# Normalization split into two pairs of row blocks, statistics products moved within attention turns, and conditioning steps moved out of a down projection

## The chip, the cores and the metric

The kernel is one program on one core of a Trainium2 chip. The core has TensorE (PE), which multiplies matrices and transposes; VectorE (DVE), ScalarE (ACT) and GpSimd (POOL) for the rest; and SyncE (SP), which here issues every DMA. The engines run their own instruction lists and wait for each other by semaphores. The metric is the device time of the whole program in microseconds (us), the median of several runs; smaller is better.

## The reference, cut to what matters

All values are fp32. The input is x of 512 rows by 1024 columns, with 256 rows of context beside it in the first half. The first half (stages `ev` and `od`) has two mixer layers; the second half has layers 0 and 1, each a mixer and a feed-forward block. Every one of the four blocks of the second half starts with a normalization that is modulated by a condition c, and ends with a gated addition:

```
adaln(c):          mod = silu(c) @ w_mod + b_mod, split into 6: shift, scale, gate for mixer and for ffn
modulate(x,g,..):  rmsnorm(x, g) * (1 + scale) + shift
ffn:               x + gate * ((silu(h @ wg) * (h @ wu)) @ wd),   h = modulate(x),  wg, wu 1024 x 2816
mixer:             x + gate * (mix(h @ w_in) @ w_out),            h = modulate(x)
```

In stage `ev`, attention B subtracts two softmaxes, and its result has an rms norm of its own over each head's 128 values (the "sub norm").

## The kernel before, in words

**Stages.** They follow each other as: norm ev, proj A, attention A, proj B, attention B, out ev, norm od, proj M, attention M, proj N, attention N, out od, norm l0m, proj S, attention S, out l0, norm l0f, ffn l0, norm l1m, proj D, attention D, out l1, norm l1f, ffn l1. A name such as l0f is the norm ahead of the feed-forward of layer 0. One function per engine (`tensor`, `scalar`, `vector`, `gpsimd`, `sync`) writes out that engine's list by hand, in that order. There is no planner: the order of the code is the order of each queue, and a wait holds all that is behind it.

**Norm of the last four blocks** (`norm_last`, `norm_mod`, `round_h`, `lower`). The output projection before it (`out_proj`, or the end of `ffn`) makes x in four row blocks t of 128 rows, in two halves of 512 columns. For each: DVE gates and adds (`add`), ACT squares with a row sum (`norm_half`), POOL makes the reciprocal root (`norm_tile`), DVE scales the row block into WK (`norm_tile`, event xn t). Then PE transposes: for each of 8 column tiles f the row blocks 0, 1, 2 into one PSUM bank (24 transposes), and after xn 3 the fourth (8 transposes). DVE applies scale and shift out of PSUM, 128x512 per f (`mod_h`); ACT rounds it to fp32r (`hh`, the high part); the low part is the difference, odd f on DVE and even f on POOL (`hl`). Each product of the second half is done in three fp32r passes: high by high, high by low weight, low by high. `fm_first` is the first product behind the norm: 32 matmuls on the high parts as they come (2 outputs, 8 f, 2 passes), then 16 on the low parts.

**Weights.** They come through a ring of 4 buffers (`load` on SP, chunk i waits until PE is done with chunk i-4). ACT rounds a chunk (`round_chunk`), DVE or POOL takes the rest (`rest`).

**Feed-forward** (`ffn`). 22 turns f of gate and up products, then the down projection in two halves hh of 512 output columns, 22 tiles f each, for 4 row blocks. ACT makes the high part of the activation (`round_a`), POOL the low part (DVE for the last four of the second half). The last six f of the second half (38 to 43 in all, "kept") are done row block by row block, so that x comes out block by block.

**Conditioning steps** (`ada`, `ADA_STEPS`). The adaln products run beside everything else in 192 small steps: "chunk" (SP loads 512 KB, DVE does four multiply-adds of 128x256), "sum", "apply" (PE broadcasts or turns the sum; for gates ACT copies it to GATE). `FFN_STEPS` gives the steps per turn: three per turn in the 22 turns of ffn l0 and three after each of the 6 chunks of the first down half; one per turn in ffn l1.

**Attention B** (`attention`, `sub_norms`). 24 units of 128 queries and two heads, one per turn. PE in turn i: scores of unit i, transposes of the probabilities of unit i-2 into PSUM banks 4 and 5, then `extra`, then the products of unit i-3, then a piece of the next gate projection as filler (`FILL`). The 8 units in `B_DONE` (3, 5, 9, 11, 15, 17, 21, 23) end a sub norm: `extra` runs `sum_squares` in turn u+5 and `spread` in turn u+6. DVE has for the first a `diagonal` (with a power on POOL in its middle), for the second two multiplications, each after that turn's maxima.

Of the kernel before, what the change touches and what calls it, by code (L numbers as in the profile page):

```python
# [291 lines left out]
FFN_STEPS = {"l0f": (3, 3), "l1f": (1, 0)}  # L292
# [4 lines left out]
def program(nc, A, out_d):  # L297
    ctx = ExitStack()
    with ctx:
# [441 lines left out]

        def attended_by(tag, u, U):
# [19 lines left out]
        VA_TILES = (4, 5, 0, 1, 2, 3)  # L762

# [66 lines left out]
        def tensor(pe):  # L830
# [59 lines left out]
            def norm_last(st, by):  # L890

                for f in range(8):
                    b = next_bank(("turn", st, f, 0), by(f, 0))
                    for t in range(3):
                        pe.wait_ge(dve_value, ("xn", st, t))
                        pe.transpose(bank(b, t * 128, (t + 1) * 128),
                                     WK[:, t * 1024 + f * 128:t * 1024 + (f + 1) * 128], ident)
                for f in range(8):
                    pe.wait_ge(dve_value, ("xn", st, 3))
                    pe.transpose(bank(where["turn", st, f, 0], 384, 512), WK[:, 3072 + f * 128:3200 + f * 128], ident)  # L900
                    pe.then_inc(pe_turned, ("turn", st, f, 0))

# [27 lines left out]
            def fm_first(st, parts):  # L930

                for i, m, tag, t, by in parts:
                    next_bank(("p", tag, t, 0), by(0))
                for k in range(8):
                    pe.wait_ge(act_value, ("hh", st, k, 0))
                    for i, m, tag, t, by in parts:
                        (Wh, Wl), b, c = split_weights(i, 8), where["p", tag, t, 0], slice(m * 128, (m + 1) * 128)
                        pe.wait_ge(rest_signal(i), ("rest", i, k // 4))
                        pe.matmul(bank(b), Wh(k, c), Hh(st, k), k == 0, False)
                        pe.matmul(bank(b), Wl(k, c), Hh(st, k), False, False)  # L940
                for i, m, tag, t, by in parts:
                    Wh, b, c = split_weights(i, 8)[0], where["p", tag, t, 0], slice(m * 128, (m + 1) * 128)
                    for k in range(8):
                        wait_h(st, k, 0)
                        pe.matmul(bank(b), Wh(k, c), Hl(st, k), False, k == 7)
# [2642 lines left out]
```

## Time and profile before

| | us |
|---|---|
| median of 3 runs (lowest, highest) | 2376.01 (2374.91, 2379.13) |
| the profiled execution | 2372.06 |
| its span, first to last instruction | 2370.3 |
| PE busy | 2278.4 (96%) |
| DVE / ACT / POOL busy | 1301.3 (55%) / 788.9 (33%) / 331.9 (14%) |
| mean granted TensorE clock | 0.994 of full |
| stretches at half clock after the first 20 us | 102.8 (3.4 long), 529.5 (3.4), 1065.3 (6.8), 1614.9 (3.4), 1642.2 (3.4), 1754.8 (3.4), 2365.8 (6.5) |
| HBM read | 221.83 MB |

Times in a trace are us from the first instruction. "PE busy" counts a matmul from start to end although matmuls overlap, so 96% busy does not mean that PE is at its peak: what counts is the distance from one start to the next.

### The profile page before, as it was taken

What the parts mean: (1) busy time and instruction counts of PE and PEld (TensorE: products, weight loads), DVE (VectorE), ACT (ScalarE), POOL (GpSimd) and SP (SyncE); (2) the same over time, 40 slices, a digit from 0 to 9 for tenths busy, and PEclk for the clock granted to TensorE, in tenths of its full rate; (3) what the DMA queues carried; (4) which work ended last, traced back from release to release, by engine and by line L of the source; (5) the groups of instructions that cost most, each with busy time, mean ns of one, the idle gap of its engine ahead of it and who ended that gap; (6) DMA issues with size and microseconds to landing.
All of it is one profiled execution on the core that took longest, in us unless ns stands there. A gap on an engine that the chain in (4) does not pass through costs nothing.

```text
span 2370.3 us, 30353 instructions
## 1 busy us (share of the span) xinstructions
PE 2278.4 (96%) x11784; PEld 1722.5 (73%) x11784; DVE 1301.3 (55%) x2871; ACT 788.9 (33%) x1675; POOL 331.9 (14%) x333
## 2 busy tenths in 40 slices
PE   7999999989999999999999999999989999999997
PEld 5866576568645667787776888887767677888876
DVE  3565655655246654657767366666358844433333
ACT  4255103431112203623557122223433642222243
POOL 2200110001000112021200110003533002000154
PEclk9999999999999999999999999999999999999999
DMA  7200331002234363022310245554322102322321
GB/s 307 72 20 35 107 107 63 18 28 72 93 111 138 90 206 92 10 89 83 107 37 2 72 157 191 185 178 164 108 76 72 54 1 89 119 95 91 105 97 72
DMA packets 58267, 225.88 MB, mean 95 GB/s; under 512 B 20478, under 2 KB 21118, under 8 KB 41740
## 3 DMA queue, kind: packets, MB, share of 16 engines
q1 hardware_dynamic: 58124, 223.94, 28.2%
q8 instruction: 93, 1.52, 0.3%
q14 instruction: 50, 0.41, 0.1%
HBM read 221.83 MB, written 2.10 MB: 94 GB/s over the span
## 4 chain that ended last, share of the span: by engine, by line
PE 87%; DVE 5%; POOL 2%; ACT 2%; issue 1%; DMA 1%; SPq 1%; POOLq 0%; ACTq 0%; DVEq 0%
PE PS L86 82%; PE PS L91 5%; POOL WKr L103 1%; ACT WK L98 1%; DVE WK L108 1%; DMA GB<-in_ev_ada 1%; DVE WK L142 1%; SPq L162 1%; ACT WK L96 1%; POOL SM L103 0%; POOL Xr L103 0%; DVE X L103 0%; DVE ACC L115 0%; DVE WK L103 0%; ACT WKr L96 0%
## 5 line engine op out<-in xcount | busy, mean ns | idle before, releaser
L86 PE MATMUL PS<-Hr,GBr 128*128 128x512 f32 x1272 | 434.8, 393 | 2.2 <-ACT Hr L96 2.2
L86 PE MATMUL PS<-Hr,RINGr 128*128 128x512 f32 (+1 forms) x1048 | 405.6, 387 | 0.0
L96 ACT ACTIVATE WK<-PS 128x512 f32<-128x512 f32 (+2 forms) x391 | 189.1, 516 | 482.0 <-PE PS L86 290.2
L86 PE MATMUL PS<-H,RING 128*128 128x512 f32 (+1 forms) x928 | 336.3, 514 | 0.0
L115 DVE SCALAR_TENSOR_TENSOR ACC<-ADA,SM,ACC 128x256 f32<-128x256 f32 x608 | 297.1, 512 | 50.0 <-DMA ADA<-in_l_mod 30.8
L86 PEld LDWEIGHTS PS<-Hr,GBr 128*128 128x128 f32 x1272 | 237.8, 188 | 55.7 <-issue 3.4
L86 PEld LDWEIGHTS PS<-H,RING 128*128 128x128 f32 x928 | 172.0, 190 | 135.1 <-issue 126.9
L103 DVE TENSOR_TENSOR RINGr<-RING,GBr 128x1024 fp32r<-128x1024 f32 x148 | 182.5, 1271 | 145.5 <-ACT GBr L96 145.5
L86 PE MATMUL PS<-RING,GB 128*128 128x256 f32 x1152 | 252.6, 381 | 3.4 <-DVE GB L120 2.2
L86 PEld LDWEIGHTS PS<-RING,GB 128*128 128x128 f32 x1152 | 219.4, 191 | 34.7 <-issue 5.0
L86 PEld LDWEIGHTS PS<-Hr,RINGr 128*128 128x128 f32 (+1 forms) x1048 | 197.2, 188 | 40.6
L96 ACT ACTIVATE GBr<-RING 128x1024 fp32r<-128x1024 f32 (+1 forms) x154 | 154.3, 1046 | 200.3 <-PE PS L86 200.3
L86 PE MATMUL PS<-GBr,WKr 128*128 128x512 f32 (+1 forms) x664 | 213.2, 391 | 7.6 <-POOL WKr L103 7.3
L91 PE MATMUL PS<-CN,WK 128*128 128x128 f32 (+1 forms) x1104 | 162.4, 281 | 23.9 <-DVE WK L108 15.5
L86 PE MATMUL PS<-GB 64*128 64x256 f32 (+5 forms) x976 | 174.8, 437 | 10.9 <-DVE GB L120 2.9
L86 PE MATMUL PS<-Xr,GBr 128*128 128x512 f32 x456 | 174.4, 389 | 2.2 <-POOL Xr L103 2.2
L91 PEld LDWEIGHTS PS<-CN,WK 128*128 128x128 f32 (+1 forms) x1104 | 118.3, 140 | 79.6 <-DVE WK L108 31.4
L86 PE MATMUL PS<-WK,GB 128*64 128x128 f32 (+2 forms) x1856 | 158.6, 280 | 0.5 <-ACT EXQ L96 0.5
L86 PEld LDWEIGHTS PS<-GBr,WKr 128*128 128x128 f32 x664 | 126.1, 190 | 41.2 <-issue 13.7
L103 POOL TENSOR_TENSOR WKr<-GB,WKr 128x512 fp32r<-128x512 f32 x76 | 108.2, 1424 | 334.2 <-ACT WKr L96 331.2
L96 ACT ACTIVATE GB<-PS 128x256 f32<-128x256 f32 (+2 forms) x88 | 43.4, 493 | 316.7 <-PE PS L86 316.5
L86 PEld LDWEIGHTS PS<-GB 64*128 64x128 f32 (+1 forms) x976 | 84.2, 187 | 81.5 <-issue 57.3
(221 smaller groups left out, 2849.0 us busy)
## 6 DMA issues: line engine op xcount, KB each, us to landing
ADA<-in_l_mod SPq DMA_DIRECT2D x96, 512.0 KB, 3.8
RING<-in_l_gu SPq DMA_DIRECT2D x44, 1024.0 KB, 4.9
RING<-in_l_wd SPq DMA_DIRECT2D x24, 1024.0 KB, 4.9
RING<-in_ev_in SPq DMA_DIRECT2D x13, 1024.0 KB, 5.6
ADA<-in_od_ada SPq DMA_DIRECT2D x24, 512.0 KB, 3.6
RING<-in_od_in SPq DMA_DIRECT2D x11, 1024.0 KB, 6.1
RING<-in_l_in SPq DMA_DIRECT2D x10, 1024.0 KB, 4.9
RING<-in_l_out SPq DMA_DIRECT2D x8, 1024.0 KB, 5.3
```

The costliest lines, as they stand in the source:

```text
L86: self.last = self.eng.matmul(out, lhsT, rhs, start=start, stop=stop, skip_group_check=True)
L91: self.last = self.eng.transpose(out, in_, ident)
L96: self.last = self.eng.activation(out, in_, func, bias=bias, scale=scale)
L98: self.last = self.eng.activation(out, in_, func, bias=bias, scale=scale, accum_out=accum)
L103: self.last = self.eng.tensor_tensor(out, a, b, op)
L108: self.last = self.eng.tensor_scalar(out, a, s1, None, op0)
L115: self.last = self.eng.scalar_tensor_tensor(out=out, in0=a, scalar=s, in1=b, op0=op0, op1=op1)
L142: self.last = self.eng.tensor_tensor_reduce(out, a, b, scale, init, op0, op1, accum)
L162: self.last = self.eng.dma_start(out, in_)
```

## The change

1. **Sub norms of attention B.** `sum_squares` and `spread` run at the end of PE's turn, one turn number lower (u+4 and u+5). On DVE their partners run at the front of the next turn, ahead of the maxima.
2. **Values of attention A.** Row block 0 is projected in turn 0, 1 in turn 1 (before: both in turn 1); 2 and 3 stay in turn 2.
3. **Norms l0m, l0f, l1m, l1f in two pairs.** Pair 0 is the row blocks 0 and 1, pair 1 the blocks 2 and 3. The 16 transposes of pair 0 go behind the third row block's output product (in ffn l0 behind the first of the last six f of row block 3). DVE's scale and shift, ACT's rounding and the low parts of pair 0 (128x256 each) are done while the fourth block is multiplied. `fm_first` then starts with the transposes of block 2, multiplies pair 0, transposes block 3, and multiplies pair 1; its 48 matmuls of 512 columns become 96 of 256.
4. **Steps.** The three steps after each of six chunks of the down projection go. 3, 2, 1 and 0 steps are put behind the row blocks of out l0 (`OUT_STEPS`). Of the steps counted through the program, 6 now run in out l0, the 22 turns of ffn l0 end at step 182 instead of 176, and the last three of the nine steps that ran in the down projection run in the first turns of ffn l1.
5. **End of the down projection.** ACT rounds the kept activations 39 to 43 together at tile 38, ahead of the last weight chunk; DVE takes their low parts ahead of that chunk's rest. In ffn l0 ACT rounds chunk `l1_qi` ahead of the four squarings, and DVE takes its rest behind the first addition.
6. The weight of the final norm of the first half is loaded to GB in place of H, since H already holds pair 0 then.

The fence below holds the core of the diff; after the two tables and PE's part come ACT's lines (from `if fz < 38`), DVE's (from `def normed`) and SP's (the last).

```
-FFN_STEPS = {"l0f": (3, 3), "l1f": (1, 0)}
+FFN_STEPS = {"l0f": 3, "l1f": 1}
+OUT_STEPS = (3, 2, 1, 0)
+        PAIRS = ((0, 256), (256, 512))
+        VA_AT = {0: (0,), 1: (1,), 2: (2, 3)}
-            return [(u, step) for u in B_DONE for step in (0, 1) if i == u + 5 + step]
+            return [(u, step) for u in B_DONE for step in (0, 1) if i == u + 4 + step]
...
+            def pair_of(st, f, g, tiles):
+                for k in (f, f + 1):
+                    for t in tiles:
                         pe.wait_ge(dve_value, ("xn", st, t))
+                        pe.transpose(bank(where["turn", st, f, g], k % 2 * 256 + t % 2 * 128, k % 2 * 256 + t % 2 * 128 + 128),
+                                     WK[:, t * 1024 + k * 128:t * 1024 + (k + 1) * 128], ident)
+            def norm_early(st):
+                for f in range(0, 8, 2):
+                    next_bank(("turn", st, f, 0), [(dve_value, ("mod_h", st, f + 1, 0))])
+                    pair_of(st, f, 0, (0, 1))
                     pe.then_inc(pe_turned, ("turn", st, f, 0))
...
             def fm_first(st, parts):
+                norm_third(st)
                 for i, m, tag, t, by in parts:
                     next_bank(("p", tag, t, 0), by(0))
+                for g, (s0, s1) in enumerate(PAIRS):
+                    for k in range(8):
+                        pe.wait_ge(act_value, ("hh", st, k, g))
...
+                            pe.matmul(bank(b, s0, s1), Wh(k, c), Hh(st, k, s0, s1), k == 0, False)
+                            pe.matmul(bank(b, s0, s1), Wl(k, c), Hh(st, k, s0, s1), False, False)
+                    if g == 0:
+                        norm_fourth(st)
                     for i, m, tag, t, by in parts:
...
+                            pe.matmul(bank(b, s0, s1), Wh(k, c), Hl(st, k, s0, s1), False, k == 7)
...
-                        if hh == 0:
-                            ada(FFN_STEPS[st][1])
...
                         down(wd, 1, f, t)
+                        if t == 3 and f == 16 and st == "l0f":
+                            norm_early("l1m")
...
-            attention("B", sub_norms, at_end)
+                sub_norms(i)
+            attention("B", None, at_end)
...
+            def then_l0f(t):
+                ada(OUT_STEPS[t])
+                if t == 2:
+                    norm_early("l0f")
+            out_proj("l0_out", range(4), lambda k, t: None, then_l0f)
...
-                            round_a(fz + 1)
+                            if fz < 38:
+                                round_a(fz + 1)
+                            elif fz == 38:
+                                for kept in range(39, 44):
+                                    round_a(kept)
...
+                    act.wait_ge(pe_product, ("a_used", wd, KEPT - 1))
+                    round_chunk(FIRST["l1_qi"])
...
+            def normed(st, t):
+                if t == 2:
+                    scaled_pair(st, 0)
+                elif t == 3:
+                    lower_pair(st, 0)
+                norm_tile(st, t)
...
-                        for z in range(40, 44):
+                        for z in range(40, 44) if hh and cj == 4 else ():
...
-            attention("B", sub_norms)
+            attention("B", front=sub_norms)
...
             ada_until(ADA_AFTER["l0m", 5])
+            for n in OUT_STEPS:
+                ada(n)
             for j in range(4):
                 load()
```

## Rows read from the trace of the kernel before

**Rows 1.** The page: the chain that ended last, shares of the span by engine.
```profile
PE 87%; DVE 5%; POOL 2%; ACT 2%; issue 1%; DMA 1%; SPq 1%; POOLq 0%; ACTq 0%; DVEq 0%
```

**Rows 2.** The chain in order of time (start, length, what): ffn l0's 22 turns.
```profile
1370.39 241.40 PE PS L86 x1088
```

**Rows 3.** Timeline (start, length), PE in proj A: two 256-column fp32r matmuls in sequence.
```profile
62.99 0.28 PE L86 MATMUL PS<-GBr,WKr 128*128 128x256 f32 x1
63.11 0.28 PE L86 MATMUL PS<-Hr,RINGr 128*128 128x256 f32 x1
```

**Rows 4.** Timeline, attention B, turns 8 and 9 ([idle before <- what ended it]).
```profile
412.06 1.56 PE L86 MATMUL PS<-GB 64*128 64x512 f32 x8 [0.51 <-ACT WK L98]
...
413.55 0.88 PE L91 MATMUL PS<-CN,WK 128*128 128x128 f32 x6
...
414.96 1.05 PE L86 MATMUL PS<-CN,GB 128*128 128x1 f32 x8 [0.53 <-ACT WK L96]
...
416.38 1.02 POOL L103 TENSOR_TENSOR SM<-SM 128x4 f32<-128x4 f32 x1 [64.51 <-DVE SM L110]
...
417.44 0.88 DVE L108 TENSOR_SCALAR GB<-CN,SM 128x128 f32<-128x128 f32 x4 [1.23 <-POOL SM L103]
...
420.40 0.88 PE L91 MATMUL PS<-CN,WK 128*128 128x128 f32 x6 [0.62 <-DVE WK L115]
...
421.83 1.10 PE L86 MATMUL PS<-GB,CN 128*128 128x512 f32 x2 [0.56 <-ACT WK L96]
...
422.97 0.75 DVE L115 SCALAR_TENSOR_TENSOR EXQ<-EXQ,SM,PS 128x512 f32<-128x512 f32 x1 [0.89 <-PE PS L86]
```

**Rows 5.** Timeline, end of out l0, norm l0f and first product of ffn l0.
```profile
1343.69 29.66 SPq L162 DMA_DIRECT2D RING<-in_l_gu  x5
...
1353.86 2.78 PE L91 MATMUL PS<-CN,WK 128*128 128x128 f32 x24
...
1358.23 1.09 PE L91 MATMUL PS<-CN,WK 128*128 128x128 f32 x8 [1.59 <-DVE WK L108]
...
1360.40 0.47 PE L86 MATMUL PS<-Hr,GBr 128*128 128x512 f32 x1 [1.08 <-ACT Hr L96]
...
1363.20 7.14 POOL L103 TENSOR_TENSOR Xr<-X,Hr 128x512 fp32r<-128x512 f32 x2
...
1370.39 0.74 PE L86 MATMUL PS<-Xr,GBr 128*128 128x512 f32 x2 [1.13 <-POOL Xr L103]
```

**Rows 6.** Timeline, norm l0m: the fourth row block's transposes.
```profile
1064.80 1.49 PE L91 MATMUL PS<-CN,WK 128*128 128x128 f32 x8 [2.92 <-DVE WK L108]
```

**Rows 7.** Timeline, norm l1m: transposes of blocks 0 to 2, and of block 3.
```profile
1748.22 2.62 PE L91 MATMUL PS<-CN,WK 128*128 128x128 f32 x22 [2.12 <-DVE WK L108]
...
1752.25 1.09 PE L91 MATMUL PS<-CN,WK 128*128 128x128 f32 x8 [1.41 <-DVE WK L108]
```

**Rows 8.** Timeline, down projection of ffn l0: its start, and its second gate step.
```profile
1614.49 0.47 PE L86 MATMUL PS<-GBr,WKr 128*128 128x512 f32 x1 [2.71 <-POOL WKr L103]
...
1639.53 0.60 ACT L96 ACTIVATE GATE<-PS 128x512 f32<-128x512 f32 x1 [2.94 <-PE PS L86]
...
1641.64 0.47 PE L86 MATMUL PS<-GBr,WKr 128*128 128x512 f32 x1 [2.15 <-POOL WKr L103]
```

**Rows 9.** Stretches: length, busy PE, PEld, DVE, ACT, POOL, clock, DMA, GB/s.
```profile
1065.40:1072.10 6.70, 5.10 (x15) 3.86 (x14) 6.61 (x10) 4.44 (x8) 3.86 (x3) 0.50 0.32 105
...
1642.20:1645.60 3.40, 3.40 (x10) 2.66 (x9) 2.88 (x2) 0.34 (x1) 0.67 (x1) 0.50 0.94 361
1754.90:1758.20 3.30, 3.30 (x9) 2.52 (x9) 3.30 (x6) 2.86 (x6) 3.11 (x3) 0.50 0.00 0
```

**Rows 10.** Timeline, down projection of ffn l0, row block 0 of the kept tiles.
```profile
1730.63 0.47 PE L86 MATMUL PS<-GBr 128*128 128x512 f32 x1 [1.80 <-DVE GBr L103]
```

**Rows 11.** Groups by form: 128x256 out of PSUM on DVE, 128x256 low parts on POOL.
```profile
L120 DVE COPY GB<-PS 128x256 f32<-128x256 f32 x22 | 9.3, 422 | 51.6 <-PE PS L86 51.6
...
L103 POOL TENSOR_TENSOR GBr<-GB,Hr 128x256 fp32r<-128x256 f32 x7 | 7.6, 1084 | 22.5 <-ACT Hr L96 22.3
```

More of the change, by code:

```diff
@@ L1192, in ffn @@
                         chunk_done(FIRST[wd] + hh * 6 + cj)
-                        if hh == 0:
-                            ada(FFN_STEPS[st][1])
-                turn["set"] = list(range(8))
+                turn["set"], turn["at"] = list(range(4)), 3
                 for t in range(4):
@@ L1553, in tensor @@
             ada_until(ADA_AFTER["l1m", 3])
-            norm_last("l1m", lambda f, gi: [(dve_value, ("mod_h", "l1m", f, gi))])
-            close(of_pe, "norm l1m")
             def weights_i():
@@ L1686, in round_h, with round_pair @@
                 round_chunk(SECOND[st])
+            def round_pair(st, g):
+                a, b = PAIRS[g]
+                for f in range(8):
+                    act.wait_ge(dve_value, ("mod_h", st, f, g))
+                    act.activation(Hh(st, f, a, b), Hl_plain(st, f, a, b), ACT.Copy)
+                    act.then_inc(act_value, ("hh", st, f, g))
+                if g:
+                    round_chunk(SECOND[st])
             def copy_out(tag, t, s0, n):
@@ L2026, in scalar @@
                     ada(1)
+                if t == 2:
+                    round_pair("l0m", 0)
             cur.allowed |= {"l0f"}
@@ L2395, in weigh, with attention @@
                         dve.then_inc(dve_probs, ("probs", tag, u))
-            def attention(tag, extra=None, behind=None):
+            def attention(tag, extra=None, behind=None, front=None):
                 units, n, lag = UNITS[tag], len(UNITS[tag]), LAG[tag]
                 for i in range(n + 6):
+                    if front is not None:
+                        front(i)
                     for t, s0, m in filled(tag, i):
@@ L2620, in sub_norms @@
             def sub_norms(i):
-                for u, step in diff_steps(i):
+                for u, step in diff_steps(i - 1):
                     t, s0, n = UNITS["B"][u]["done"]
@@ L2885, in vector, with normed_with_steps @@
             since(dve, "att S")
-            out_proj("l0_out", "l0m", range(4), ("c2",), lambda t: norm_tile("l0f", t), "l0_gu")
+            def normed_with_steps(t):
+                normed("l0f", t)
+                ada(OUT_STEPS[t])
+            out_proj("l0_out", "l0m", range(4), ("c2",), normed_with_steps, "l0_gu")
             cur.allowed |= {"l1m"}
@@ L2890, in vector @@
             since(dve, "out l0")
-            ffn("l0f", "l0_gu", "l0_wd", lambda t: norm_tile("l1m", t))
+            ffn("l0f", "l0_gu", "l0_wd", lambda t: normed("l1m", t))
             cur.allowed |= {"l1f"}
@@ L2951, in vector @@
             since(dve, "att D")
-            out_proj("l1_out", "l1m", range(4), ("c2",), lambda t: norm_tile("l1f", t), "l1_gu")
+            out_proj("l1_out", "l1m", range(4), ("c2",), lambda t: normed("l1f", t), "l1_gu")
             close(of_dve, "out l1")
@@ L3216, in gpsimd, with then_l1m @@
             since(pool, "out l0")
-            ffn("l0f", "l0_gu", "l0_wd", lambda t: norm_tile("l1m", t))
+            def then_l1m(t):
+                norm_tile("l1m", t)
+                if t == 2:
+                    lower_pair("l1m", 0)
+            ffn("l0f", "l0_gu", "l0_wd", then_l1m)
             cur.allowed |= {"l1f"}
```

188 lines of the change are left out of this document (100 added, 88 removed).

## The prediction

> **What bounds the kernel now.** First the page: the chain that ended last is 87% TensorE, then DVE with 5% [rows 1]. So the time is PE's instruction list plus its waits, and a part of the change is worth what it takes from either. Then the chain in order of time, which gives PE's undisturbed rate: 1088 matmuls in 241.40 us, 0.222 us each [rows 2]. Against that rate I walked PE's starts through the whole trace and kept every distance that is too long. They lie in few places, and for these I read the timeline. The reader is to see three things there.
>
> (a) Each of the four late norms makes PE wait three times: for the fourth row block's xn (1.59 us idle), for the first rounded tile (1.08), and for POOL's low parts (1.13) [rows 5]; l1f repeats this to 0.03 us. (b) Where PE's work gets thin, the granted clock falls to half: 6.7 us in norm l0m, 3.3 to 3.4 us in l1m and at the second gate step of ffn l0's down projection [rows 9]. A half-clock stretch costs half of PE's busy time in it. (c) In attention B the small products of the sub norm wait 0.53 and 0.56 us behind ACT's copy of the transposes issued just before them, since both use banks 4 and 5 [rows 4].
>
> A wait costs more than its idle time: the last matmul's tail and the slow first one (0.47 long against 0.39) add about 0.2 to 0.25 us.
>
> **Sub norms of attention B.** The six transposes start at 413.55, 0.11 apart, so PE could go on at 414.25; it goes on at 414.96 [rows 4]: 0.7 lost. The starts before spread lose 0.72 to 0.78. Units 3 to 17 give 12 such waits, 8.7 us; units 21 and 23 fall into turns whose order stays the same. At the end of the turn the filler (1.9 us) has let ACT empty the banks, so these waits go. Beside this, scores wait 0.51 for the exponentials once in six turns [rows 4], where sum_squares will now stand: 3 x 0.67 = 2.0 more. And PE's wait of 0.62 for DVE's probabilities [rows 4], three times, should go as DVE no longer idles for the late sum: 1.8.
> What is added: DVE now has the diagonal ahead of the maxima. Queued behind it are the gate, the maxima and the weighing; ACT's exponentials wait for the maxima, and the next scores for ACT. The diagonal takes 0.2 + 1.02 on POOL + 0.2 + 0.88, the other half 0.75 + 0.69 (the add behind it) [rows 4]. Laying turns 8 and 9 out by hand, DVE ends its maxima 2 to 3 us later, and the next scores come 0.6 to 1 us late. I take 3.5 us for all. Nothing in the trace shows this order, so the bounds are 0 and 8.5. **Gain 8.7 + 2.0 + 1.8 - 3.5 = 9.0** (4 to 12.5).
>
> **Attention A.** 24 matmuls move from turn 1 to turn 0; PE has no long wait in either. Transposes come next in both orders after DVE has long made the probabilities. **0** (-0.5 to 0.5).
>
> **The four norms.** Before, the waits cost 1.59 + 1.08 + 1.13 and three times 0.23: **4.5 us** each in l0f and l1f. In l0m: 2.92 [rows 6], 1.6 idle in the half-clock stretch, 5.10/2 for its busy part [rows 9], 0.5 for the restarts: **7.5**. In l1m: 2.12 and 1.41 [rows 7], 1.07, 3.3/2 [rows 9], 0.7: **7.0**. Together 23.5.
> After: 32 transposes remain, 16 of them ahead of the fourth block's product, 0.11 each as now (2.78 for 24) [rows 5]; they move and cost nothing new. From the end E of the output product PE has block 2's transposes (0.9) and 32 matmuls of 256 columns. These start 0.12 apart [rows 3], so 3.85: PE is busy to E + 4.75, and xn 3 comes at E + 4.6 (1353.6 to 1358.2 in rows 5). The first wait is covered. Then the low products (1.9) cover DVE's and ACT's first tile of pair 1 (0.42 + 0.4) [rows 11], so the second goes too. The costs that take their place:
> - 96 x 0.12 = 11.5 in place of 48 x 0.222 = 10.7: 0.8 in each norm.
> - POOL's last low part. Before, two took 7.14 us where 2.6 would do [rows 5]: while DVE subtracted and took the chunk's rest, POOL's stood still, and it ended 1.1 after DVE's last. Now it starts about when DVE's own low parts start. If it gets ahead of them nothing is lost; if it falls behind the rest again, PE waits about 1.4. I take 0.7 in each norm.
> - l0f: SP now waits at block 2 for a conditioning chunk on DVE, which is behind eight scalings (8 x 0.42), a norm_tile (0.8) and four multiply-adds (2.0): from 1341.7 to 1348.2. Queued behind that wait is the first load of l0_gu, issued at 1343.69 now [rows 5]. It lands near 1353.2, ACT rounds it, DVE's rest comes ahead of the last addition, and xn 3 is 0.7 late.
> - l0m: the same eight scalings sit ahead of norm, final norm and a chunk; the last additions slip 1 us and the low parts of pair 0 0.2: 1.2.
> - l1m: the early transposes need xn 1 while PE reaches them 0.7 us after block 2's product; DVE and ACT are held by chunk l1_qi, which lands about 1732.4. I count 0.8 there and 0.3 for xn 2.
>
> So l1f 4.5 - 1.5 = 3.0; l0f 2.3; l0m 7.5 - 2.7 = 4.8; l1m 7.0 - 2.6 = 4.4. **Gain 14.5** (10 with POOL at its worst and 1.5 for other slips; 20.3 with the 0.8 alone).
>
> **Steps.** Counting the steps through the program, the gate applied in the down projection behind its second chunk is l1m 5. ACT cannot round on before it has copied this gate, which PE makes only then: ACT idles 2.94, PE 2.15 [rows 8]. With the restart and 3.4/2 for the half clock [rows 9] that is **4.0** (2.4 if the clock falls anyway). The wait at the projection's start has the same mechanism, 2.71 [rows 8], but there the count puts a gate into the 22nd turn in both kernels (l1m 4 before, l1m 5 after), so it stays. The other moved work is DVE's and SP's, covered by 5 us of DVE idle per half block of out l0 and by the turns of ffn l1; uncovered it would be at most 1 us. The applications cost PE the same elsewhere.
>
> **Kept tiles.** PE waits 1.80 [rows 10] as DVE's low parts stand behind the last chunk's rest, and ACT's roundings behind its chunk. Reordered, they are ready 2 us before they are needed, and the rest, at 1729.9, comes in time for tile 42. 2.05 in each of two projections: **4.1** (3 to 4.1). Next late is nothing of PE's.
>
> **Sum.** 9.0 + 14.5 + 4.0 + 4.1 = 31.6. The profiled execution took 2372.1 (its span and 1.8): 2340.5. The median of the runs is 3.9 above it, so 2376.0 - 31.6 = **2344 us**.
>
> **Rivals.**
> 1. *The chain through attention B eats its gain.* For it: scores already wait for ACT once in six turns. Against it: DVE's idle time there. Gain there 1 in place of 9: **2352**.
> 2. *POOL is locked out wholly.* The rows speak for it: POOL ended its last low part 1.1 us after DVE's last subtraction. The same in each of four norms costs another 0.7: 2344 + 2.8 = **2347**. By the Trainium skill, "SBUF — State Buffer", section "SBUF: two separate sides", a DVE operation with two SBUF inputs and a GpSimd operation hold a shared pair of ports exclusively, so that the later one blocks for the whole instruction. By that rule, the trace agrees (7.14 for two), and this rival is the case in which DVE always starts first.
> 3. *The start of the down projection is cured too*, by a gate copy that comes earlier: 2.71, restart and 3.4/2 of clock, 4.6 more: **2339**. Against it: the count of steps. Its opposite is the change not doing what it says: gates still copied between chunks.
> 4. *Slower.* DVE's diagonal and its second half lie open on the loop scores, maxima, exponentials, scores: 2.3 + 1.44 = 3.8 us at each of 8 units, 30 us, against a gain of 22.6 elsewhere: +7.8, **2384**. It decides from 2.8 us per unit. Against it: the tail's units are not in the loop, and DVE is 67% busy there (88.6 of 133 us).
>
> **How the numbers follow.** Forecast 0.63, rival 1 0.15, rival 2 0.12, rival 3 0.08, rival 4 0.02. The range takes the bounds of the terms, not all at once: gains of 16 (rival 1's 1 in attention B, norms 10, the rest 5.4) to 43. So 2333 to 2360, which holds rivals 1 to 3. A measurement of this kernel can tell about 0.2%, 4.8 us, from no change. Only rival 4 and a third of the outer misses reach that side: faster 0.94, same 0.03, slower 0.03.
>
> **What would show it.** In the changed kernel's profile: no half-clock stretch in l0m, l1m and behind the second chunk of ffn l0's down projection, but one near its start with some 2.7 us of idle; matmuls of 256 columns 0.12 apart behind each norm, with a wait before POOL's last low part under 1.5; CN,GB and GB,CN products in attention B without an ACT wait, its 133 us stretch about 124; no 1.8 us wait in the kept tiles. Wrong would be: 256-column matmuls that start 0.19 apart (the length of a weight load), scores waiting over 1 us in turns u+6, or the first row block's chain in ffn l0's end late by more than the 4.1 us that a block takes.

## The result, and the profile after

| | before | changed |
|---|---|---|
| median (lowest, highest), 4 runs each | 2375.46 (2372.75, 2379.13) | 2336.89 (2335.19, 2341.98) |
| the profiled execution, its span | 2372.06, 2370.3 | 2341.98, 2340.2 |
| mean granted TensorE clock, profiled | 0.994 | 0.994 |

The ratio is 0.984, 95% interval 0.9819 to 0.9861: 38.6 us less. Timed again, beside other kernels, it gave 2338.34 against 2371.21, ratio 0.9849 (0.9827 to 0.9872). The forecast was 2344, a ratio of 0.9867: direction and range hold, and the gain is some 4 to 7 us larger than forecast. The changed kernel's profiled execution is the longest of its four, so the two traces differ by 30.1 only; why is shown below.

**Where the time went.** I measured between the same matmuls in every trace: each mark is the start of the last matmul ahead of a long distance that all traces have at that place. Times in us; e1, e2 and e7 are runs described below.

| from, to | before | changed | changed again (e7) | attention B alone (e1) | norms undone (e2) |
|---|---|---|---|---|---|
| end of norm ev, attention B | 325.71 | 325.74 | 324.12 | 331.73 | 331.74 |
| attention B | 152.89 | 140.65 | 140.67 | 140.64 | 140.68 |
| its end, attention M | 202.56 | 202.56 | 202.56 | 202.55 | 202.55 |
| attention M, attention N | 186.76 | 189.74 | 186.45 | 186.67 | 186.45 |
| attention N, out od | 87.57 | 87.73 | 87.82 | 87.70 | 88.69 |
| out od, norm l0m, attention S | 195.76 | 193.03 | 193.07 | 195.36 | 196.46 |
| attention S | 99.95 | 99.88 | 99.88 | 99.94 | 99.96 |
| out l0, norm l0f, ffn l0 to its down projection | 314.02 | 313.26 | 313.21 | 313.99 | 316.93 |
| down projection, norm l1m, to attention D | 246.16 | 235.34 | 235.25 | 245.88 | 237.85 |
| attention D to the end | 512.96 | 505.86 | 505.84 | 512.85 | 510.77 |

The chain of the page answers to [rows 1], and the long chain of ffn l0 to [rows 2]. Here the chain could be followed back to 1350 us only, so its shares are of 42% of the span and say little against before's.

```profile
PE 38%; POOL 2%; DVE 1%; ACT 1%; issue 0%; DMA 0%; POOLq 0%; ACTq 0%; DVEq 0%
```

Attention B, turns 8 and 9, timeline (start, length, engine, line, operation, [idle before <- what ended it]):

```profile
411.88 0.95 PE L86 MATMUL PS<-CN,GB 128*128 128x1 f32 x8
...
412.75 1.56 PE L86 MATMUL PS<-GB 64*128 64x512 f32 x8
...
413.63 1.02 POOL L103 TENSOR_TENSOR SM<-SM 128x4 f32<-128x4 f32 x1 [61.28 <-DVE SM L110]
414.25 0.87 PE L91 MATMUL PS<-CN,WK 128*128 128x128 f32 x6
414.69 0.88 DVE L108 TENSOR_SCALAR GB<-CN,SM 128x128 f32<-128x128 f32 x4 [1.23 <-POOL SM L103]
...
416.21 1.99 PE L86 MATMUL PS<-H,RING 128*128 128x256 f32 x8 [0.65 <-DVE GB L115]
...
418.04 1.02 PE L86 MATMUL PS<-GB,CN 128*128 128x512 f32 x2
419.08 1.56 PE L86 MATMUL PS<-GB 64*128 64x512 f32 x8
...
420.57 0.87 PE L91 MATMUL PS<-CN,WK 128*128 128x128 f32 x6
```

Against [rows 4] the three waits for ACT and the one for DVE's probabilities are gone. One new wait came: the filler at 416.21 waits 0.65 for DVE's gate, which now stands behind the diagonal. Scores (419.08) come without a wait. Six turns, from scores to scores, took 34.91 us in the trace of before (407.46 to 442.37) and take 31.18 here (407.95 to 439.13).

Norm l0m, timeline of DVE and PE around the fourth row block (against [rows 6]):

```profile
1051.59 1.23 DVE L103 TENSOR_TENSOR RINGr<-RING,WKr 128x1024 fp32r<-128x1024 f32 x1 [1.74 <-ACT WKr L96]
1052.24 1.04 PE L91 MATMUL PS<-CN,WK 128*128 128x128 f32 x8
1052.73 1.22 DVE L103 TENSOR_TENSOR RINGr<-RING,GBr 128x1024 fp32r<-128x1024 f32 x1
1053.87 0.68 DVE L103 TENSOR_TENSOR WK<-PS,GATE 128x512 f32<-128x512 f32 x1
...
1059.41 1.09 PE L91 MATMUL PS<-CN,WK 128*128 128x128 f32 x8 [2.31 <-DVE WK L108]
```

The output product ends at 1052.2, but DVE first takes the rest of the next weight chunk, so the last gated addition starts at 1053.87 and xn 3 is 2.31 us late. In this trace the granted clock then falls to half from 1060.4 for 3.4 us. The six traces with this same code and this same wait (2.30 to 2.34) do not agree on that: the fall comes in the changed kernel, e4 and e7, and not in e3, e6 and e11. First the changed kernel, then e3 (length, busy PE, PEld, DVE, ACT, POOL, clock, DMA, GB/s):

```profile
1060.40:1063.80 3.40, 3.40 (x18) 3.40 (x18) 3.31 (x8) 2.19 (x6) 1.52 (x3) 0.50 0.52 158
```

```profile
1055.40:1058.80 3.40, 3.40 (x31) 3.40 (x30) 3.31 (x8) 2.16 (x6) 1.49 (x3) 1.00 0.52 130
```

From out od to attention S it takes 192.96 to 193.07 us with the fall and 191.53 to 191.57 without it.

Norm l0f (against [rows 5]):

```profile
1345.34 2.36 DVE L103 TENSOR_TENSOR RINGr<-RING,GBr 128x1024 fp32r<-128x1024 f32 x2 [5.55 <-ACT GBr L96]
...
1346.71 0.36 PE L86 MATMUL PS<-Hr,GBr 128*128 128x256 f32 x1 [0.59 <-DVE RINGr L103]
...
1352.06 1.09 PE L91 MATMUL PS<-CN,WK 128*128 128x128 f32 x8 [1.28 <-DVE WK L108]
...
1355.59 0.75 POOL L103 TENSOR_TENSOR Xr<-X,Hr 128x256 fp32r<-128x256 f32 x1
1356.27 0.75 DVE L103 TENSOR_TENSOR Hr<-H,Hr 128x256 fp32r<-128x256 f32 x2
1356.49 1.81 POOL L103 TENSOR_TENSOR Xr<-X,Hr 128x256 fp32r<-128x256 f32 x1 [0.16 <-ACT Hr L96]
```

The waits for the first rounded tile and for the low parts are gone, as forecast; a short one for the weight's rest came, and the one for xn 3 stayed. POOL has three of its four low parts done when DVE's begin.

Norm l1m (against [rows 7]) and the start of the down projection of ffn l0 (against [rows 8]):

```profile
1599.63 0.60 ACT L96 ACTIVATE GATE<-PS 128x512 f32<-128x512 f32 x1 [5.70 <-PE PS L86]
1599.71 0.53 POOL L125 MEMSET ACC<- 128x512 f32 x1 [22.14 <-PE PS L86]
1600.12 1.14 ACT L96 ACTIVATE WKr<-GB 128x512 fp32r<-128x512 f32 x2
...
1602.30 0.47 PE L86 MATMUL PS<-GBr,WKr 128*128 128x512 f32 x1 [2.71 <-POOL WKr L103]
...
1725.33 1.86 PE L91 MATMUL PS<-CN,WK 128*128 128x128 f32 x15 [1.18 <-DVE WK L108]
...
1730.94 1.09 PE L91 MATMUL PS<-CN,WK 128*128 128x128 f32 x8 [0.32 <-DVE WK L108]
```

The second gate's wait between chunks is gone and the first one, 2.71, is still there, both as forecast. The kept tiles (against [rows 10]): DVE's four low parts now begin 3.5 us before PE comes to the kept tiles, and PE finds no wait there.

```profile
1707.44 4.67 DVE L103 TENSOR_TENSOR GBr<-GB,GBr 128x512 fp32r<-128x512 f32 x4 [3.39 <-ACT GBr L96]
...
1710.91 0.39 PE L86 MATMUL PS<-GBr 128*128 128x512 f32 x1
```

**The clock as an account of its own.** Each run comes with its mean granted clock, to 0.001. Where PE is busy throughout, a stretch at half clock costs half its length (128x512 matmuls start 0.43 apart at 1643 us of before's trace, 0.22 to 0.23 at full clock) and lowers the mean by the same share, so time x clock is the time at full clock. Where PE waits inside such a stretch, this counts the clock too high. For each kernel I take the mean over its runs; rounding moves a single run by up to 1.2 us, and the mean of several by less.

| kernel | runs | mean us | at full clock | the clock's cost |
|---|---|---|---|---|
| before, in three groups of runs | 11, 17, 11 | 2373.2, 2372.9, 2374.1 | 2356.2, 2355.9, 2355.8 | 17.0, 17.0, 18.3 |
| changed, in two groups | 4, 5 | 2337.7, 2338.2 | 2326.6, 2327.4 | 11.1, 10.8 |
| e1 attention B alone | 5 | 2362.5 | 2344.0 | 18.5 |
| e2 norms and values undone | 6 | 2359.5 | 2336.7 | 22.8 |
| e3 kept order undone | 4 | 2342.2 | 2332.3 | 9.9 |
| e4 no steps in turn 21 | 4 | 2330.3 | 2323.9 | 6.4 |
| e5 values alone | 12 | 2372.1 | 2355.1 | 17.0 |
| e6 values undone | 5 | 2344.2 | 2328.3 | 15.9 |
| e8 three cures | 4 | 2325.6 | 2321.0 | 4.6 |
| e9 round first | 5 | 2333.3 | 2325.9 | 7.4 |
| e10 attention B and values | 6 | 2358.7 | 2343.0 | 15.7 |
| e11 steps (3, 0, 0, 0) | 4 | 2329.4 | 2321.8 | 7.6 |
| e12 two cures | 4 | 2326.5 | 2320.6 | 5.9 |

The means at full clock repeat to 0.4 us for the kernel before and to 0.8 for the changed one; most of what varies between executions of one kernel is the clock's part (17 runs of before: standard deviation 4.3 us as timed, 1.4 at full clock). A mean of the clock's part over five or six runs can be 1 to 2 us off. The change gains 29 us of the first kind and 6 of the second.

### The profile page after: what moved, and what is told of

Its sections match the earlier page's. It is cut to its first block and busy times, and to the rows that moved or that the text cites. A ratio compares the mean times of both kernels' runs of the same rounds, so it can differ in the third digit from the quotient of the medians.

```text
span 2340.2 us, 30852 instructions
## 1 busy us (share of the span) xinstructions
PE 2274.7 (97%) x11976; PEld 1732.8 (74%) x11976; DVE 1309.9 (56%) x2919; ACT 795.4 (34%) x1707; POOL 326.5 (14%) x349
## 5 line engine op out<-in xcount | busy, mean ns | idle before, releaser
L86 PE MATMUL PS<-Hr,GBr 128*128 128x512 f32 (+1 forms) x1332 | 440.6, 384 | 0.6 <-DVE RINGr L103 0.6
L86 PEld LDWEIGHTS PS<-Hr,GBr 128*128 128x128 f32 x1332 | 247.7, 188 | 51.7 <-issue 3.9
L86 PEld LDWEIGHTS PS<-Hr,RINGr 128*128 128x128 f32 x1112 | 208.9, 188 | 38.0
L91 PE MATMUL PS<-CN,WK 128*128 128x128 f32 (+1 forms) x1104 | 163.2, 282 | 16.6 <-DVE WK L108 11.1
L86 PE MATMUL PS<-Xr,GBr 128*128 128x512 f32 (+2 forms) x484 | 176.1, 378 | 0.0
L86 PEld LDWEIGHTS PS<-WK,GB 128*64 128x64 f32 (+2 forms) x1856 | 126.9, 149 | 21.3 <-issue 20.2
```

What stands on the lines that cost most here:

```text
L86: self.last = self.eng.matmul(out, lhsT, rhs, start=start, stop=stop, skip_group_check=True)
L91: self.last = self.eng.transpose(out, in_, ident)
```

## The experiments

Ratios are to the kernel before, timed in the same group of runs on the same chip.

**e1: part 1 alone** (put on the kernel before: `u + 4 + step`, PE's `sub_norms(i)` at the turn's end, DVE's at its front).

> The kernel before with part 1 of the change alone (attention B's sub norms at the end of PE's turn, their DVE halves at the front of the next). Theory: this part alone takes the 12.2 us that the two traces show between the start of attention B and its end (372.15 to 512.81 in place of 371.67 to 524.56), because DVE had room for the diagonal ahead of the maxima. So the ratio to the kernel before is 0.995 (12 us less), no stretch outside attention B changes, and DVE's diagonal makes no score late. Rival: only the 9.0 us of the prediction belong to it and the other 3 come from part 2 or from the neighbours; then 9 us less.

Measured: 2361.58, ratio 0.9954 (0.9938 to 0.997), 11 us. Attention B takes 140.64 us in place of 152.89, to 0.03 us what the changed kernel takes, and no other stretch changes by its own work. At full clock 2356.2 - 2344.0 = 12.2. The theory holds, the 9.0 does not. Its trace shows one thing beside it: 331.73 us up to attention B in place of 325.71, with half clock from 104 to 121 us, in a stretch that part 1 does not touch. That led to e5 and e6.

**e2: norms undone** (the kernel before with parts 1 and 4, and of part 5 the kept tiles; the earlier rounding of chunk `l1_qi` is not in it and so counts with the norms here).

> The kernel before with parts 1, 4 and 5 (sub norms, steps, kept tiles), without the norms in pairs and without part 2. What the changed kernel gains beyond this one is the norms' share. Theory: the traces put 2.7 (l0m) + 0.8 (l0f) + some 3 to 5 each for l1m and l1f on the norms, so this kernel is 10 to 12 us slower than the changed one: 22 to 26 us faster than the kernel before, ratio 0.989 to 0.991. POOL's last low part in l0f is again over 5 us long, since DVE's subtractions run beside it. Rival: the prediction's 14.5 us for the norms stand, and this kernel is 17 to 19 us faster than before, with steps and kept tiles worth less than 8 together.

Measured: 2361.67, ratio 0.9939 (0.9922 to 0.9957), 14.5 us by the ratio, 13.7 by the means: both expectations miss. At full clock the kernel is 19.5 us under the kernel before, close to the rival's 17 to 19; the clock took 5.8 of them back. In its trace the steps behind out l0 leave less cover to the old norm l0f: the wait for the fourth row block grows from 1.59 [rows 5] to 2.88, and 6.8 us at half clock begin in it, at 1356.8.

```profile
1358.22 1.97 PE L91 MATMUL PS<-CN,WK 128*128 128x128 f32 x8 [2.88 <-DVE WK L108]
...
1363.33 7.17 POOL L103 TENSOR_TENSOR Xr<-X,Hr 128x512 fp32r<-128x512 f32 x2
```

So the parts lean on each other: moving the steps cost 2.9 us there (314.02 to 316.93) and the norms in pairs took it back. Changed against e2, trace by trace, the norms give 3.4 (l0m), 3.7 (l0f), 2.5 (l1m) and 4.9 (l1f: 3.9 by the first turns of ffn l1, and 1.0 scattered over what follows), together 14.5; at full clock 2336.7 - 0.9 (part 2) - 2327.0 = 8.8. The norms alone lie between e2 and e6 (below), which differ in nothing else: 2359.5 - 2344.2 = 15.3 by the means, of which 8.4 at full clock and 6.9 of the clock.

**e3: order of the kept tiles undone.**

```
-                            if fz < 38:
-                                round_a(fz + 1)
-                            elif fz == 38:
-                                for kept in range(39, 44):
-                                    round_a(kept)
+                            round_a(fz + 1)
```

and DVE's four low parts go back behind the last chunk's rest.

> The changed kernel with the kept tiles rounded one by one behind the last weight chunk, as before (part 5's first half undone). Theory: PE waits 1.8 us ahead of tile 40 in both projections again, 2.05 us with the restart, so 4.1 us slower than the changed kernel: ratio to before 0.986 where the changed one has 0.984. Rival: the late roundings make row block 0 late once and the early transposes of l1m hide it, so in ffn l0 nothing shows: 2 us.

Measured: 2342.2, ratio 0.9869 (0.9852 to 0.9885), 4.7 us over the changed kernel's 0.9849 of another group of runs. The intervals of the two overlap; what carries the reading is the traces, against e7 2.85 us more from the down projection to attention D and 2.02 more from there to the end, and the 4.9 us at full clock. The wait of 1.80 is back in both projections; the rival falls.

```profile
1707.78 0.47 PE L86 MATMUL PS<-GBr 128*128 128x512 f32 x1 [1.80 <-DVE GBr L103]
```

**e4: no steps in turn 21 of ffn l0** (`ada(FFN_STEPS[st] if (st, f) != ("l0f", 21) else 0)` on every engine).

> The changed kernel with no conditioning steps in the last of the 22 turns of ffn l0. The gate l1m 5 is then copied behind attention D. Theory: the wait of 2.71 us at the start of the down projection exists because ACT copies this gate, and POOL clears the sum, ahead of rounding the first activation. Without it PE goes on without a wait, and with its restart and half of the 3.4 us at half clock that is 4.6 us less than the changed kernel: ratio to before about 0.982. The gate's application at the end of attention D costs up to 1 us there. Rival: the first activation is late for its own reasons (the last tanh, the last product, POOL's low part of 1.35 us), and the wait stays above 1.5 us with the gate gone; then under 1 us less.

Measured: 2330.56, ratio 0.9818 (0.9803 to 0.9834). ACT now rounds the first activation right behind its own work, 4.7 us ahead of PE, and PE waits for nothing:

```profile
1586.77 1.14 ACT L96 ACTIVATE WKr<-GB 128x512 fp32r<-128x512 f32 x2
1587.54 2.97 POOL L103 TENSOR_TENSOR WKr<-GB,WKr 128x512 fp32r<-128x512 f32 x2 [17.02 <-ACT WKr L96]
1591.52 0.39 PE L86 MATMUL PS<-GBr,WKr 128*128 128x512 f32 x1
```

From the end of attention S to attention D it takes 542.71 in place of 548.59, 5.9 less, and from there to the end 0.98 more, where the gate's application now stands: 4.9 net. Against the changed kernel's 0.9849 of another group the ratios give 7 us, of which 3.5 are at full clock (2327.4 - 2323.9). The theory holds.

**e5 and e6: part 2 alone, and undone** (`VA_AT` and its three uses).

> The kernel before with part 2 alone: row block 0 of attention A's values is projected in turn 0. Theory (new): the prediction's 0 was wrong. PE is busy for 3.32 us of the stretch 100 to 105 in the kernel before and for 4.94 in the changed one; where it is thin the granted clock falls to half, for 3.4 us in the one trace and for 17.1 us in the traces of the two runs with part 2 undone. So with this part alone the start of attention B comes 2 to 7 us earlier than without it, no trace shows a half-clock stretch between 100 and 125 us, and the median is 3 to 6 us under the kernel before's. Rival: the half-clock stretches fall anywhere by chance, and the ratio is 1.000 within its interval.

> The changed kernel with part 2 undone. Theory: a half-clock stretch of 3.4 to 17 us at 100 to 122 us comes back, and the median is 3 to 6 us over the changed kernel's of the same call; the spread of its runs grows from about 2 to about 8 us. Rival: no difference beyond 1 us.

Measured: e5 2371.21, ratio 0.9996 (0.9982 to 1.001) in 12 runs; e6 2344.93, ratio 0.9874 (0.9852 to 0.9896), against 0.9849 for the changed kernel beside it, 6.6 us by the medians. The stretches of the trace (length, busy PE, PEld, DVE, ACT, POOL, granted clock, DMA, GB/s), first with part 2 undone (e6), then the changed kernel again (e7), then part 2 alone (e5):

```profile
100.00:105.00 5.00, 3.26 (x27) 2.86 (x28) 1.92 (x7) 2.17 (x7) 0.00 (x0) 0.85 0.00 0
105.00:110.00 5.00, 5.00 (x28) 4.72 (x26) 3.11 (x10) 2.10 (x6) 0.00 (x0) 0.50 0.02 3
```

```profile
100.00:105.00 5.00, 4.94 (x48) 4.57 (x48) 1.92 (x7) 2.45 (x8) 0.00 (x0) 1.00 0.01 3
105.00:110.00 5.00, 5.00 (x55) 4.60 (x51) 3.31 (x11) 2.10 (x6) 0.00 (x0) 1.00 0.00 0
```

```profile
100.00:105.00 5.00, 4.94 (x47) 4.64 (x47) 1.63 (x5) 0.72 (x2) 0.00 (x0) 1.00 0.00 0
```

PE was idle for a third of the stretch before the fall without part 2, and 28 matmuls run in 5 us in place of 55. The idle time is a single wait: the scores wait 1.68 us for DVE's row maxima. It stands in all four traces without part 2, and the half clock begins within 0.3 us of its end. With part 2 the 24 matmuls of row block 0 stand in its place. The timeline of before, then of e7:

```profile
99.73 1.15 PE L86 MATMUL PS<-GB 64*128 64x256 f32 x12
...
102.56 2.33 PE L86 MATMUL PS<-GB 64*128 64x128 f32 x16 [1.68 <-DVE SM L142]
```

```profile
100.62 1.15 PE L86 MATMUL PS<-GB 64*128 64x256 f32 x12
101.70 0.33 PE L86 MATMUL PS<-GATEr,Hr 128*128 128x128 f32 x1
...
104.52 1.37 PE L86 MATMUL PS<-GB 64*128 64x128 f32 x16
```

In the four traces without part 2 the way to attention B is 325.71 once and 331.7 three times; in the ten with it 322.5 to 325.7, 323.6 on the mean: 322.5 where no half-clock stretch lies on the way, and two of 3.4 us (at 50.1 and 128.6) in the first trace of the changed kernel, which is why its 325.74 looks like before's. Two more waits, 1.03 and 1.62 us ahead of transposes of later turns, stand between 122 and 129 us in both kernels' traces. So in the traces part 2 is worth 6.6 us, and on the changed kernel 6.1 on the mean (6.6 by medians), 0.9 of it at full clock. But on the kernel before it gained nothing beyond the noise: 0.8 at full clock, and the clock's cost of 17.0 is the same. The one trace of e5 has half-clock stretches at 49.9 and 930.5 us that the trace of before lacks; whether the fall moves there in general is not shown.

**e7: the changed kernel again.**

> The changed kernel itself, unchanged, as the yardstick for its variants on this chip, and for what its trace owed to chance. Theory: the first trace's extra 3.0 us between 715 and 905 us (a conditioning chunk that landed late, and a half-clock stretch behind it) do not come back, and the median is 2333 to 2338. Rival: they belong to the change and come back.

Measured: 2338.34 (2336.9 to 2339.44), ratio 0.9849 (0.9827 to 0.9872). Between attention M and N it takes 186.45 in place of 189.74: the 3.0 us over the kernel before's 186.76 were chance. They came once more in the fourteen traces, in e10 (189.72), again with half clock in that stretch. The median lies 0.3 over the range that was expected.

**e8: the waits that were left.** On the changed kernel:

```
-OUT_STEPS = (3, 2, 1, 0)
+OUT_STEPS = (3, 0, 0, 0)
...
-                        if t == 3 and f == 16 and st == "l0f":
+                        if t == 3 and f == 18 and st == "l0f":
...
                 for jj in range(2):
+                    if t == 3 and jj == 0:
+                        round_chunk(FIRST["l0_in1"])
                     act.wait_ge(dve_value, ("x", "od_out", t, jj))
...
-                    if t == 3 and jj == 0:
-                        round_chunk(FIRST["l0_in1"])
...
-                norm_half("l0f", t, 0, "l0_out")
                 if t == 3:
                     round_chunk(FIRST["l0_gu"])
+                norm_half("l0f", t, 0, "l0_out")
```

> The changed kernel with four edits aimed at the waits that its trace still shows: steps (3, 0, 0, 0) behind out l0, so that the last turn of ffn l0 has no gate and the first load of l0_gu is not held; ACT rounds the first chunk of the next product ahead of the last row block's squares in out od and out l0, so that DVE's rest stands no longer between it and the last addition; the early transposes of l1m two tiles later. Theory: start of the down projection 4.6 less 1.0 at the end of attention D; xn 3 of l0m 1.4 us earlier, of l0f 0.7 to 1.4 with the 0.6 wait for the rest; l1m 1.3. Sum 7.5 to 9.5 us under the changed kernel of this call. Rival: the waits move on to the next late thing (ACT's squares, POOL's root) and only the 3.6 of the gate remain.

Measured: 2325.9 (2324.38 to 2326.4), ratio 0.9796 (0.9774 to 0.9818), 12.4 us under the changed kernel beside it: 6.4 at full clock, 6.2 of the clock. The forecast of 7.5 to 9.5 left out part of the clock's gain. In norm l0f no wait over 0.4 us is left. In l1m one is, longer than before the edit and now for another row block:

```profile
1714.34 1.09 PE L91 MATMUL PS<-CN,WK 128*128 128x128 f32 x8 [1.67 <-DVE WK L108]
```

**e9: the chunk rounded first, in out od alone.**

> The changed kernel with one edit: in out od ACT rounds chunk l0_in1 ahead of the squares of the last row block's first half, not behind them. Theory: xn 3 of l0m is late because DVE's rest of this chunk (2.4 us) stands between the last product and the last addition, which the changed kernel's trace shows at 1053.87 with the product over at 1052.2. The wait of 2.3 us ahead of the fourth row block's transposes falls to 0.9, and with PE busier no half-clock stretch follows it, so 1.4 + 1.7 = 3.1 us under the changed kernel. Rival: the stretch at half clock comes anyway (it has come in three of four traces of changed kernels), and only 1.4 us are gained.

Measured: 2333.55 (2329.96 to 2336.91), ratio 0.9822 (0.9798 to 0.9847). DVE has the rest done before the product ends, and starts the last addition 0.3 us behind it:

```profile
1049.16 1.22 DVE L103 TENSOR_TENSOR RINGr<-RING,GBr 128x1024 fp32r<-128x1024 f32 x1
...
1050.71 0.69 DVE L103 TENSOR_TENSOR WK<-PS,GATE 128x512 f32<-128x512 f32 x1 [0.33 <-PE PS L86]
1055.45 0.75 DVE L108 TENSOR_SCALAR WK<-WK,SM 128x1024 f32<-128x1024 f32 x1 [1.26 <-POOL SM L103]
1056.26 1.09 PE L91 MATMUL PS<-CN,WK 128*128 128x128 f32 x8 [0.89 <-DVE WK L108]
```

The wait is 0.89 in place of 2.31, and no half clock follows. From out od to attention S it takes 190.12 in place of 193.07: 2.95, where 3.1 was expected. Only 1.4 of it is the edit's own: e3, e6 and e11, with the old wait and no half clock behind it, take 191.55. The other 1.5 is a half-clock stretch that came in three of the six traces with the old wait and in none of the three with the short one (e8, e9, e12); that leans to the theory and does not show that the edit removes it. The runs agree on the first part: 0.7 and 1.5 us at full clock, by the two groups of the changed kernel. Over the whole the medians give 4.8 us and the ratios 6; what is beyond this stretch is the clock elsewhere.

**e10: parts 1 and 2.**

> The kernel before with parts 1 and 2. Theory: part 2 is worth 6 us on the changed kernel and nothing on the kernel before; if it needs part 1's denser attention B to keep its gain, this kernel is 16 to 19 us faster than the kernel before, ratio 0.992 to 0.993, where part 1 alone gave 0.9954. Rival: part 2's gain on the changed kernel has to do with the later parts or with chance, and this kernel stands at 0.995 as part 1 alone.

Measured: 2359.48, ratio 0.9933 (0.9913 to 0.9953) against 0.9954 for part 1 alone. 5 us by the ratios, 3.8 by the means, 1.0 at full clock. That is just short of the 0.992 to 0.993 that was expected, and the intervals overlap (0.9938 to 0.997 for part 1 alone), so this leans to the theory and does not settle it.

**e11: the steps alone.**

> The changed kernel with one number changed: the steps behind the row blocks of out l0 are (3, 0, 0, 0) in place of (3, 2, 1, 0). It does two things: the last gate leaves turn 21 (4.9 us less, as the run without steps in turn 21 showed), and the first load of l0_gu no longer stands behind a conditioning chunk. Theory: the second is worth the 0.6 to 0.8 us that PE waits for DVE's rest in norm l0f and half of the 1.4 before the fourth block's transposes, so this kernel is 6.3 us under the changed one, 1.4 under the one without steps in turn 21. Rival: the rest still stands ahead of the last addition, and nothing is gained beyond the 4.9.

Measured: 2329.64, ratio 0.981 (0.9787 to 0.9833), against the changed kernel's 0.9849 some 9 us where 6.3 was expected, 5.6 of it at full clock (2327.4 - 2321.8); about 2 us under e4 by the ratio and 2.1 at full clock (2323.9 - 2321.8), where 1.4 was expected. With this edit alone both waits of norm l0f fall under 0.4 us. SP was what held the chunk of l0_gu, not ACT's order. In the trace of e9, whose steps are (3, 2, 1, 0), PE waits 0.65 and 1.28, in the changed kernel's 0.59 and 1.28.

**e12: e8 without the later transposes.**

> The run with three cures, less the later early transposes of l1m, which go back to the first of the last six tiles. Theory: that edit only moved PE's wait from xn 1 (1.3 us) to xn 2 (1.8 us), since DVE's eight scalings begin later and stand ahead of xn 2; so this kernel is equal or up to 0.6 us faster than the 2325.9 of that run, relative to the kernel before the same 0.9796 or a little less. Rival: the shift had gained its 1.3 us and the wait for xn 2 has another cause; then this one is about 1 us slower.

Measured: 2326.47, ratio 0.9797 (0.9774 to 0.982): the same as e8. The early transposes wait 1.15 for xn 1 and 0.31 for xn 2, where e8 waits for xn 2 alone. The wait had moved.

```profile
1709.01 1.86 PE L91 MATMUL PS<-CN,WK 128*128 128x128 f32 x15 [1.15 <-DVE WK L108]
...
1714.62 1.09 PE L91 MATMUL PS<-CN,WK 128*128 128x128 f32 x8 [0.31 <-DVE WK L108]
```

e8 and e12 are the fastest kernels here, 2.0% under the kernel before.

## Why the prediction was right, point by point

The forecast's own sum, split into work and clock (3.4/2 and 5.10/2 where its steps counted them), against what the runs give:

| step of the prediction | forecast, of it clock | measured at full clock | by |
|---|---|---|---|
| sub norms of attention B | 9.0, 0 | 12.2 | e1 |
| attention A | 0, 0 | 0.9 | e5, e6, e10 |
| the four norms | 14.5, 4.2 | 8.8 | e2, e7 |
| steps | 4.0, 1.7 | 2.4 | e1, e2, less kept |
| kept tiles | 4.1, 0 | 4.9 | e3, e7 |
| sum | 31.6, 5.9 | 29.2, and about 6 of clock | |

Without its clock the forecast holds 25.7 us of work; 29.2 were measured. The 5.9 of clock agrees with the measured 6, but not term by term: by the means the clock's cost goes from 17.0 to 18.5 with part 1 (e1), to 22.8 with steps and kept tiles (e2), down to 15.9 with the norms (e6) and to 11 with part 2 (e7). That the sum of these comes out near 5.9 is luck.

- **What bounds the kernel, and the reading by starts: right.** Every gain lies in a place where the distance between two starts had been too long. But the list of such places had a hole: attention A's.
- **Attention B: mechanism right, size 3.2 too small.** The failed term is the 3.5 us for DVE's longer chain. Laid out by hand it made the next scores 0.6 to 1 late; in the trace scores wait only twice, at the stage's start and as before (0.93 and 0.87), and the price is the filler's wait of 0.60 to 0.65, three times. The tail, counted at nothing as its order stays, gave another 1.1 us. Rivals 1 and 4 (DVE's chain eats the gain) are refuted: the stretch takes 140.62 to 140.68 us in all twelve traces with part 1.
- **Attention A: the step that failed.** "PE has no long wait in either" was the argument for 0, and it is false: in the kernel before the scores wait 1.68 us for DVE, up to 102.56, just where the 24 matmuls were moved to. They fill that wait, and the half-clock stretch that stands behind it in all four traces without part 2 is in none of the ten with it. The work is worth 0.8 to 1.0 us in the runs at full clock (e5, e6, e10) and 1.5 in the traces, where the way to attention B is 322.5 with no half clock in it and before's 325.71 less half of 3.4 is 324.0. What the clock adds is 5 us on the changed kernel (e6, e7) and nothing that can be seen on the kernel before (e5); why they differ stays open.
- **The norms: sum near, in part by luck, shares wrong.** Against e2 the traces give 14.5 and the means 15.3 (e6), forecast 14.5. But of work it is 8.4 to 8.8 where 10.3 was forecast, and of clock 6.9 where 4.2 was; l0f's 3.7 holds a half-clock stretch of e2's trace that before's lacks. l1f gave 3.9 by the first turns of ffn l1, where 3.0 was forecast: of the costs set against it, POOL's 0.7 did not come, for POOL was three low parts ahead of DVE when DVE began. l0m gave 2.7 against the kernel before in place of 4.8. The failed step is xn 3 "at E + 4.6", read from l0f and used for all four: l0m makes two norms, and in the trace of before its xn 3 lies 5.6 behind the product's end (1059.10 to 1064.74), which the cover of 4.75 does not reach. With the slip that was forecast at 1 and measured at 1.5 it waits 2.31, and in this trace a half-clock stretch stayed, against the first sign that the prediction named. Where it did not come (e3, e6, e11) l0m gave 4.2. e9 removes 1.4 of the wait. l1m gave 2.5 between these traces, and 4.2 with the 1.7 of a half-clock stretch at the start of the down projection that e2's trace lacks; 4.4 was forecast, with 0.8 for early transposes that wait 1.18.
- **Rival 2, POOL locked out: refuted as a cost.** The mechanism is there (next section), and the order took it off the path.
- **Steps: right.** At the second chunk the wait of 2.15 us is gone (0.17 is left), and the wait at the start is there to 0.01 us (2.71). Rival 3, the start cured too, did not happen by itself; e4 and e11 are that rival made true, and it is worth 4.9 in e4's trace, where 4.6 was forecast. The 1.7 of clock in this term is not seen in the runs, where e2's clock costs 4.3 more than e1's; in e2's trace the stretch at the second chunk is gone and the one of 6.8 us in l0f has come. What the forecast lacked is that l0f pays for the steps: 2.9 with the old norm (e2), 2 with the new one (e11), of which the 0.7 for xn 3 had been counted and the wait for the rest had not.
- **Kept tiles: right**, 4.1 forecast, 4.9 by the traces and at full clock, 4.7 by the ratios.
- **The total** came out 4 to 7 us low. By the account of the means it is 4: attention B 3.2, attention A 0.9 and the kept tiles 0.8 of work more than forecast, the norms 1.5 less, and under 1 of clock; the rest of the first ratio's 38.6 is the spread of the groups of runs. The range's upper gain, 43, is more than its terms give: their written bounds add up to 12.5 + 0.5 + 20.3 + 4.0 + 4.1 = 41.4; the result lies inside either. The profiled executions differ by 30.1 only, since the changed kernel's had 3.0 us of chance and the kernel before's one of the better clocks: the median of the runs and the sum made on one execution stood 3.9 apart before, and 5.1 the other way after.

## What to carry to other kernels

When you go through a trace for the waits of the bounding engine, check the list against the granted clock: look for the wait ahead of each stretch at half clock. Here the stretch at 102.8 us stood in the table, and the wait of 1.68 us that ended at 102.56 was on no list. Such a stretch can cost more than the wait itself, and it comes in some executions and not in others, so take the time at full clock and the clock's cost apart, and do not credit an edit with a stretch that one trace lacks. When a wait stays after its cause was removed, read what the releasing engine does between the product's end and the late operation; here it was the next weight's rest, and moving the rounding that feeds it by one operation was worth 1.4 us. A step moved out of one stage loads the cover of another, so measure the edits together and apart.

## What the runs showed of the hardware that was not expected

- The clock's part of the time varies between executions of one kernel and is a property of the kernel too: on the mean 17 to 18 us for the kernel before, 11 for the changed one, 5 to 6 for e8 and e12. After the same wait of 1.68 us it stayed at half for 3.4 us in one trace (before, at 102.8) and for 17.1 in three (e1, e2, e6), with PE busy for 13.50 of the last 13.50 us of it. After the same wait of 2.3 us in norm l0m it fell in three traces and not in three others.
- POOL's subtraction of 128x256 takes 0.74 to 0.75 us alone and 1.81 when DVE subtracts beside it; its 128x512 takes 1.30 alone and, as the last of [rows 5], 5.71 beside six subtractions of DVE in a row (7.14 for the two). By the Trainium skill, "SBUF — State Buffer", section "SBUF: two separate sides", the two engines hold a shared pair of ports exclusively for a whole instruction; by that rule, the trace agrees. With smaller tiles POOL had three of its four done before DVE's began, and lost 1.1 us once, off the path, in place of 4.4 on it; DVE's next operation, a 128x1024 rest at 1357.78, took 1.60 where the one behind it took 1.21.
- 256-column fp32r products start 0.12 us apart over whole sequences of 32 in the norms (0.121 to 0.122 on the mean in the changed kernel's trace), as the two of [rows 3] had suggested.
